# The expert's second matrix as one sum of 512 columns, and a second layer that starts with the high parts

## The reference

```python
def expert_block(args):
    xblk, e = args
    return (jax.nn.silu(xblk @ w1[e]) * (xblk @ w3[e])) @ w2[e]
```

## Time and profile before

| what | value |
|---|---|
| median of 3 runs | 950.17 us (949.08 to 951.76) |
| span of the profiled execution | 950.5 us |
| PE busy | 890.4 us, 94% |
| DVE busy | 633.5 us, 67% |
| ACT busy | 404.7 us, 43% |
| POOL busy | 196.5 us, 21% |
| PE on the chain that ended last | 43% of the span |
| passes of 256 columns for the second matrix | 1104, about 0.28 us each as shown, overlapping |
| weight loads | 48 of 2 MB, 13.7 us from issue to landing (median) |

### The profile page before, as it was taken

One profiled execution on the slowest core, in us unless ns is written; L12 is line 12 of the kernel. 1 busy time (PEld: TensorE's weight loads), 2 busy tenths in 40 slices (PEclk: granted clock), 3 DMA queues, 4 the chain that ended last, 5 costly groups with the idle time before them and its releaser, 6 DMA issues.

```text
span 950.5 us, 15781 instructions
## 1 busy us (share of the span) xinstructions
PE 890.4 (94%) x5739; PEld 756.8 (80%) x5740; DVE 633.5 (67%) x876; ACT 404.7 (43%) x559; POOL 196.5 (21%) x216
## 2 busy tenths in 40 slices
PE   4989999999999999999999999999999999999880
PEld 1788877888897577887888988988898898888770
DVE  1567555689867547455875759499845746799934
ACT  3573375301224432221421556377543533677721
POOL 4231000000000010110001323233513313244233
PEclk9898999999999999999979999999999999999985
DMA  9845445502034033122947769889989669699765
GB/s 340 308 139 160 140 134 174 181 13 68 20 134 178 3 131 111 67 90 89 335 172 249 248 181 335 270 270 378 377 260 326 198 177 307 196 356 359 284 210 221
DMA packets 81254, 194.55 MB, mean 205 GB/s; under 512 B 4043, under 2 KB 12400, under 8 KB 81211
## 3 DMA queue, kind: packets, MB, share of 16 engines
q1 hardware_dynamic: 70624, 158.87, 47.6%
q0 software_dynamic: 7712, 25.10, 10.7%
q10 hardware_dynamic: 2874, 10.01, 2.7%
HBM read 168.53 MB, written 25.71 MB: 204 GB/s over the span
## 4 chain that ended last, share of the span: by engine, by line
PE 43%; DVE 4%; DMA 2%; issue 1%; ACT 1%; POOL 0%; DVEq 0%; ACTq 0%; POOLq 0%; SPq 0%
PE ps L2019 26%; PE ps L2030 9%; PE ps L2035 4%; PE ps L2013 2%; DMA raw<-in_w_dram 2%; DVE arena L1601 1%; PE ps L2002 1%; PE ps L2069 1%; PE ps L2048 0%; PE ps L1953 0%; DMA out_dram<-arena 0%; DVE onehot L1506 0%; DVE w1l L1542 0%; ACT arena L1062 0%; PE ps L1998 0%
## 5 line engine op out<-in xcount | busy, mean ns | idle before, releaser
L2019 PE MATMUL ps<-w3h,xTh 128*128 128x256 f32 x368 | 105.9, 288 | 0.0
L2019 PE MATMUL ps<-w3h,xTl 128*128 128x256 f32 x368 | 104.1, 283 | 0.0
L2019 PE MATMUL ps<-w3l,xTh 128*128 128x256 f32 x368 | 104.1, 283 | 0.0
L1542 DVE TENSOR_TENSOR w1l<-raw,w1h 128x2048 fp32r<-128x2048 f32 x30 | 68.6, 2287 | 28.4 <-ACT w1h L988 28.4
L988 ACT ACTIVATE w1h<-raw 128x2048 fp32r (+1 forms) x32 | 61.1, 1912 | 57.9 <-PE ps L2035 39.4
L2019 PE MATMUL ps<-w2h,hTh 128*128 128x512 f32 x184 | 76.9, 418 | 1.0 <-DVE hTl L1555 0.5
L2030 PE MATMUL ps<-w1h,xTh 128*128 128x512 f32 x184 | 73.0, 397 | 3.7 <-issue 3.4
L988 ACT ACTIVATE w2h<-raw 128x2048 fp32r (+1 forms) x32 | 61.1, 1918 | 31.5 <-PE ps L2019 22.7
L2030 PE MATMUL ps<-w1l,xTh 128*128 128x512 f32 x184 | 72.8, 395 | 0.0
L2019 PE MATMUL ps<-w2l,hTh 128*128 128x512 f32 x184 | 72.2, 393 | 0.0
L2019 PE MATMUL ps<-w2h,hTl 128*128 128x512 f32 x184 | 72.1, 392 | 0.0
(11 more groups left out here) (349 smaller groups left out, 2215.6 us busy)
## 6 DMA issues: line engine op xcount, KB each, us to landing
raw<-in_w_dram SPq DMA_DIRECT2D x48, 2048.0 KB, 13.7
arena<-in_w_mod_dram SPq DMA_DIRECT2D x32, 512.0 KB, 3.8
arena<-in_x_dram SPq DMA_DIRECT2D x16, 512.0 KB, 9.5
arena<-in_w_in_dram SPq DMA_DIRECT2D x8, 1024.0 KB, 6.3
arena<-in_w_mod_dram SPq DMA_DIRECT2D x3, 2048.0 KB, 13.5
x_rows<-arena ACTq DMA_DIRECT2D x9, 512.0 KB, 3.2
hx_rows<-arena ACTq DMA_DIRECT2D x9, 512.0 KB, 4.2
wo_f<-in_w_out_dram SPq DMA_DIRECT2D x2, 2048.0 KB, 8.6
```

The costliest lines, as they stand in the source:

```text
L1542: dve.tensor_tensor(half_of(j, w_lo[j][:, :], k), half_of(j, raw[:, bass.ds(base, UNIT)], k), half_of(j, w_hi[j][:, :], k).bitcast(F32), A ...
L2019: ins = pe.matmul(out_ap, parts[l][:, lhs], w_parts[w][:, cols], start=start and n == 0, stop=stop and n == 2)
```

## The change

- The second matrix becomes one sum of 512 columns into bank 3: 24 passes instead of 48. `l1b` is now given when half of the depth is through, `l1c` when all is. w3 is split by halves of the depth, as w1 and w2 are.
- Both halves of the product of gate and up wait for `l1c`. Both now read bank 3.
- PE turns six tiles of the next rows, waits for the first half of `hid`, turns it (bank 5), turns the last two tiles, and waits for `hTh_a` (the high part) instead of `hT_a`.
- The second layer goes by halves of its depth: eight passes on the high part of `hid`, then (in the first half) the turns of the second half of `hid` into bank 4, then four passes on its low part.
- DVE makes in a splitting block low(0) for both halves, then both products, then both low parts of the turned half, and only then low(1, first half). ACT copies the two turned halves around `turn_out` and the second half of w3 behind both.

```diff
         def half_of(j, unit, k):
-            if j == 1:
-                return unit.rearrange("p (k n) -> p k n", k=KC)[:, :, k * 256:(k + 1) * 256]
             return unit[:, k * (UNIT // 2):(k + 1) * (UNIT // 2)]
...
                             high(1, place[1] * UNIT, 0)
-                            hidden_high(b, 0)
                             act.wait_ge(S["l1c"], b + 1)
                             act.sem_inc(S["load_seen"], 1)
-                            high(1, place[1] * UNIT, 1)
+                            hidden_high(b, 0)
                             turn_out(b + 1)
                             hidden_high(b, 1)
+                            high(1, place[1] * UNIT, 1)
...
             def hidden(b, k):
                 if k == 0:
                     dve.wait_ge(S["silu_done"], b + 1)
-                dve.wait_ge(S["l1c" if k else "l1b"], b + 1)
-                dve.tensor_tensor(hid[:, k * 256:(k + 1) * 256], hsil[:, k * 256:(k + 1) * 256], ps[:, 3 + k, 0:256], ALU.mult)\
+                    dve.wait_ge(S["l1c"], b + 1)
+                dve.tensor_tensor(hid[:, k * 256:(k + 1) * 256], hsil[:, k * 256:(k + 1) * 256], ps[:, 3, k * 256:(k + 1) * 256], ALU.mult)\
                     .then_inc(S["hid_b" if k else "hid_a"], 1)
...
                             low(0, place[0] * UNIT, e + 1, 0)
+                            low(0, place[0] * UNIT, e + 1, 1)
                             hidden(b, 0)
-                            low(0, place[0] * UNIT, e + 1, 1)
+                            hidden(b, 1)
                             hidden_low(b, 0)
-                            hidden(b, 1)
+                            hidden_low(b, 1)
                             low(1, place[1] * UNIT, e + 1, 0)
-                            hidden_low(b, 1)
                             turn_out(b + 1)
                             low(1, place[1] * UNIT, e + 1, 1)
                             weigh(b, s, pair)
...
             for k in range(2):
                 hidden(last, k)
+            for k in range(2):
                 hidden_low(last, k)
...
                 for q, done in enumerate(("l1b", "l1c")):
-                    for k in range(KC):
-                        if k == 0:
-                            pe.wait_ge(w_split[1], 2 * e + (q + 1))
-                        col = k * HALF + q * 256
-                        ins = product(ps[:, 3 + q, 0:256], x_parts, slice(k * P, (k + 1) * P), (w3h, w3l),
-                                      slice(col, col + 256), k == 0, k == KC - 1)
-                        if q == 1 and k == 3:
-                            pe.wait_ge(S["hid_a"], b + 1)
-                            for m in range(2):
-                                h_ins = pe.transpose(ps[:, 5, m * P:(m + 1) * P], hid[:, m * P:(m + 1) * P], ident[:, :])
-                            h_ins.then_inc(S["hta"], 1)
+                    pe.wait_ge(w_split[1], 2 * e + (q + 1))
+                    for k in range(4 * q, 4 * q + 4):
+                        ins = product(ps[:, 3, :], x_parts, slice(k * P, (k + 1) * P), (w3h, w3l),
+                                      slice(k * HALF, (k + 1) * HALF), k == 0, k == KC - 1)
                     ins.then_inc(S[done], 1)
                 if more:
-                    turn_block(b + 1)
-                pe.wait_ge(S["hT_a"], b + 1)
+                    turn_block(b + 1, 0, 6)
+                pe.wait_ge(S["hid_a"], b + 1)
+                for m in range(2):
+                    h_ins = pe.transpose(ps[:, 5, m * P:(m + 1) * P], hid[:, m * P:(m + 1) * P], ident[:, :])
+                h_ins.then_inc(S["hta"], 1)
+                if more:
+                    turn_block(b + 1, 6, KC)
+                pe.wait_ge(S["hTh_a"], b + 1)
                 pe.wait_ge(S["y_ready"], y_count)
-                for k in range(4):
-                    if k % 2 == 0:
-                        pe.wait_ge(w_split[2], 2 * e + (k // 2 + 1))
-                    if k == 2:
-                        pe.wait_ge(S["hT_b"], b + 1)
-                    for h in range(2):
-                        col = k * D + h * HALF
-                        ins = product(ps[:, 6 + h, :], h_parts, slice(k * P, (k + 1) * P), (w2h, w2l),
-                                      slice(col, col + HALF), k == 0, k == 3)
-                    if k == 1:
-                        ins.then_inc(S["l2_half"], 1)
-                    if k == 0:
+                for k0 in (0, 2):
+                    pe.wait_ge(w_split[2], 2 * e + (k0 // 2 + 1))
+                    if k0 == 2:
+                        pe.wait_ge(S["hTh_b"], b + 1)
+                    for k in range(k0, k0 + 2):
+                        for h in range(2):
+                            for w in (w2h, w2l):
+                                pe.matmul(ps[:, 6 + h, :], hTh[:, k * P:(k + 1) * P], w[:, k * D + h * HALF:k * D + (h + 1) * HALF],
+                                          start=(k == 0 and w is w2h), stop=False)
+                    if k0 == 0:
                         pe.wait_ge(S["hid_b"], b + 1)
                         for m in range(2):
-                            h_ins = pe.transpose(ps[:, 5, (2 + m) * P:(3 + m) * P], hid[:, (2 + m) * P:(3 + m) * P], ident[:, :])
+                            h_ins = pe.transpose(ps[:, 4, m * P:(m + 1) * P], hid[:, (2 + m) * P:(3 + m) * P], ident[:, :])
                         h_ins.then_inc(S["htb"], 1)
+                    pe.wait_ge(S["hT_b" if k0 else "hT_a"], b + 1)
+                    for k in range(k0, k0 + 2):
+                        for h in range(2):
+                            ins = pe.matmul(ps[:, 6 + h, :], hTl[:, k * P:(k + 1) * P], w2h[:, k * D + h * HALF:k * D + (h + 1) * HALF],
+                                            start=False, stop=(k == 3))
+                    if k0 == 0:
+                        ins.then_inc(S["l2_half"], 1)
                 ins.then_inc(S["l2_done"], 1)
```

More of the change, by code:

```diff
@@ L1007, in hidden_high @@
                 act.wait_ge(S["htb" if k else "hta"], b + 1)
-                act.activation(hTh[:, k * 256:(k + 1) * 256], ps[:, 5, k * 256:(k + 1) * 256], ACT.Copy)\
+                act.activation(hTh[:, k * 256:(k + 1) * 256], ps[:, 5 - k, 0:256], ACT.Copy)\
                     .then_inc(S["hTh_b" if k else "hTh_a"], 1)
@@ L1554, in hidden_low @@
                 dve.wait_ge(S["hTh_b" if k else "hTh_a"], b + 1)
-                dve.tensor_tensor(hTl[:, cols], ps[:, 5, cols], hTh[:, cols].bitcast(F32), ALU.subtract)\
+                dve.tensor_tensor(hTl[:, cols], ps[:, 5 - k, 0:256], hTh[:, cols].bitcast(F32), ALU.subtract)\
                     .then_inc(S["hT_b" if k else "hT_a"], 1)
@@ L2008, in _, with turn_block @@
             pe.sem_inc(S["y_ready"], 2)
-            def turn_block(b):
-                pe.wait_ge(S["gathered"], 16 * b + 16)
-                for k in range(KC):
+            def turn_block(b, first=0, end=KC):
+                if first == 0:
+                    pe.wait_ge(S["gathered"], 16 * b + 16)
+                for k in range(first, end):
                     ins = pe.transpose(ps[:, k // 4, (k % 4) * P:(k % 4 + 1) * P], xg[:, k * P:(k + 1) * P], ident[:, :])
-                ins.then_inc(S["x_turned"], 1)
+                if end == KC:
+                    ins.then_inc(S["x_turned"], 1)
             def product(out_ap, parts, lhs, w_parts, cols, start, stop):
```

## The result

The changed kernel takes 977.55 us (median of 4 runs, 975.86 to 980.5) against 950.23 us (949.08 to 951.76): ratio 1.028, 95% interval 1.026 to 1.031, so 27 us slower. The forecast was 972.5, 958 to 985. The profiled execution has a span of 974.0 us, and its own device time was 975.86, the lowest of the four. In every run that lists both, of either kernel, the device time is 1.7 to 1.9 us above the span. So the profiled execution before, span 950.5, took some 952.3 us by an estimate from these runs, 2 us over its median, and the spans differ by 23.5 us where the medians differ by 27.3.

What follows compares the result with a forecast made beforehand. PE, DVE and weight loads were nearly level in the runs; DVE would then pace eight rounds. Span 950.5 +14.7 +2.1 -0.5 +1.8 +4.4 = 973.0, so 972.5 us of device time, range 958 to 985.

Steps and rivals of the forecast that it cites:

- DVE's serial round: Between two splitting blocks DVE's in-order work takes 4.13 + 16.02 = 20.15 us against 18.31 now; eight times, +14.7 us.
- PE's own rounds: Where nothing else binds, a round is 18.30 us; seven rounds that split nothing grow 0.3 each, +2.1 us.
- The tail: Last block: the second copy comes 9.42 us after the second sum's start, was 7.61; final norm's squares follow it, +1.8 us.
- block 21's wait: Block 21's extra PE wait of 0.50 us, going back to a late w3, goes away: -0.5 us.
- The clock: PE's waits in the eight rounds drop the granted clock in every second one, at 1.1 us each: +4.4 us.
- Span and device time: From a span of 973.0 us, 0.3 off and the last halves rounded down gave 972.5 us of device time.
- (a): Rival: PE goes on setting the pace and DVE keeps up, all rounds 18.3, 953.6 us; chance 0.10.
- (c): Rival: the half clock becomes the rule, drops hit all high passes, 981 and up to 988 us; chance 0.12.
- The pass price: Second matrix: a 512-column pass costs 0.227 us by the rows, so 24 take 5.44, a gain of 0.31 per block.
- (b): Rival: PE's waits close as well, a round is PE's bare 17.63, 939 to 942 us; chance 0.07 together with (d).
- (d): Rival: the reordering does nothing, only 0.31 us a block is gained, 943 us; chance 0.07 together with (b).
- What I made of the formula: Second matrix: by the skill's formula the gain would be 0.06 us, and the sum 22 x 0.25 = 5 us higher.

Runs made afterwards that it cites:

- experiment 1: The changed kernel with the first w3 split on DVE moved between the two low parts of the turned half: 957.81 us, ratio 1.008 to the kernel before.
- experiment 5: The kernel before with two lines of DVE's order exchanged, the first w3 split behind the second low part: 962.06 us, ratio 1.012.
- experiment 6: The changed kernel once more, unaltered, for a second profile: 978.32 us, span 974.7.
- experiment 3: The kernel before with only the second layer's passes on the high parts first, two sums and DVE's and ScalarE's orders kept: 947.92 us, ratio 0.9964.
- experiment 2: The changed kernel with the second layer's passes in the old order, waiting for the low part first: 980.94 us, ratio 1.031 to the kernel before.
- experiments 4: The changed kernel with the second half's split of w1 moved behind the two products of gate and up: 963.05 us, ratio 1.012 to the kernel before.

## Why the prediction was right, step by step

**DVE's serial round.** Confirmed, by taking it away (experiment 1) and by making it alone (experiment 5). It was worked out as 4.13 + 16.02 = 20.15 us and is 4.32 + 16.13 = 20.45 in the round shown, 20.34 to 20.48 in all eight. The term was 8 x 1.84 = 14.7, each round going from 18.31 to 20.15. The rounds show +15.8, and it would be +16.8 if one of them (19.22) hadn't held 0.9 us of late weights before, which the term left out. I was 0.19 short on the way to the second low part: the eight high passes take 1.93 us from the first's start to the turns behind them (664.21 to 666.14) where I had 8 x 0.227 = 1.81, and ScalarE's copy starts 0.48 behind turns that followed a wait, not 0.41.

**PE's own rounds.** The mechanism is right, the size was too small: 18.53 us, not 18.30. By the starts of its instructions in the round of block 10, the way from the product to the first high pass takes 1.58 us where I had 1.49, and from there to the end of the second layer's first half it is 3.05 (703.10 to 706.15) where I had 1.81 + 0.22 + 0.91 = 2.94: the passes start again behind a wait, and I priced them as in a full stream. Over thirteen rounds that is +5.1 instead of the 2.1 of the sum. This is the term that was most off in share.

**The tail.** Expected +1.8 for the last block, and -0.5 for block 21's wait, together +1.3; measured from block 21's product on +1.8. It hangs on another thing than I said, though. ScalarE's timeline in the changed kernel, answering to the earlier trace rows:

```profile
941.78 0.38 ACT L1006 ACTIVATE hTh<-ps 128x256 fp32r<-128x256 f32 x1 [2.59 <-PE ps L2067]
942.41 1.06 ACT L1060 ACTIVATE arena<-arena 128x1024 f32<-128x1024 f32 x1 [0.24 <-DMA arena<-x_rows]
...
947.40 1.06 ACT L1060 ACTIVATE arena<-arena 128x1024 f32<-128x1024 f32 x1 [1.08 <-DMA arena<-x_rows]
```

The squares wait for the rows' landing, not for the copy. By the chain of waits, that landing goes back over the adding of block 21's rows (10.74 us of transfer) to its weighing on DVE, which stands ten microseconds behind the block's product, behind two splits of w3. That the sizes are near each other is chance. In experiment 6, the same kernel, this stretch is only 0.6 us longer than before, with 9.81 us for that transfer; in experiment 1, with the same last block, it is 1.1 us shorter (58.2), and there the squares start behind the copy without a wait.

**The clock.** Four falls at 1.1 us were taken; the two profiles show one each behind the eight waits, at 1.6 and 1.5. The price of a fall that meets the high passes was right at its upper end, the number too high: 2 of 16 waits of some 1.8 us were followed by one, and 2 of 8 of some 1.35 with one of 0.9 behind them. The Trainium skill (TensorE: Matmul & The Clock Gate, HAM oscillation) tells of a kernel whose clock fell in every tile, but behind waits of 3 to 5 us. The trace agrees with it where PE stands idle that long, between blocks 21 and 22:

```profile
923.72 0.77 PE L2031 MATMUL ps<-w1h,xTh 128*128 128x512 f32 x1 [3.29 <-issue]
```

There the granted clock is 0.50, the 1.2 GHz level, from 923.0 to 929.8, and all eight profiles have such a fall at this place. The timed runs of the changed kernel lie 1 to 4.6 us above its profiled one, with mean granted clocks of 0.964 to 0.969 against 0.976. That mean takes in the other stages and doesn't tell of falls in the rounds: the profile of experiment 6 has 0.968 with one fall there, that of the kernel before 0.964 with none. Whether the slower runs hold more falls stays open.

**Span and device time.** I put the device time 0.3 us under the span, because I held the span of one execution against the median of others. It stands 1.7 to 1.9 above the span in every run, 1.86 in the profiled one. That alone is 2.2 of the 5.0 us between forecast and median; 1.7 more is that the profiled execution was the fastest of its four. The span itself was forecast at 973.0 and is 974.0. Its errors mostly cancel: -0.8 on where the stage begins, +1.1 on the eight rounds, +3.0 on the others, -2.8 on the clock, +0.5 behind block 21's product. So that the span came within 1 us is luck; that DVE paces the eight rounds isn't.

**The rivals.** PE keeping the pace (a) holds in the thirteen other rounds and fails in the eight. The half clock as the rule (c) fails: seven of eight waits in each profile pass without a fall. (b) and (d) fail: the wait for the copy shows as 10.5 us idle on PE ahead of the first high passes, x184, in the page's group of L2062. The pass price taken from the rows holds, 5.44 for 24. The formula of the Trainium skill (TensorE: Matmul & The Clock Gate, Back-to-back issue gap) gives 215.8 ns for 512 columns, and the chain shows 227. The same section has about 131 ns for 512 columns in a stream with its weight loads; no pass here comes near that. What I made of the formula was also counted wrong: 22 x 0.25 is 5.5, and only the fourteen rounds that DVE doesn't pace could carry it, 3.5 us.

**What the change is made of.** The single sum gains 0.31 us of passes per block and loses the cover of the product, copy and turn. Even with DVE's order mended, the kernel with the single sum is 957.8 against 951.7 (experiment 1), and 9.9 us above experiment 3, which has the high parts first but two sums and the old orders: 18.53 us a round against 18.00. No run has the single sum alone. The high parts first gain 3.8 us on the kernel before (experiment 3) and 2.6 or 3.4 on the changed one (experiment 2). DVE's order loses some 20 us (experiment 1), falls of the clock among it. The part worth keeping is the second one, at 947.9 us.

## What to carry to other kernels

An engine that works 17.4 us of an 18.3 us round has under 1 us to spare, even when it is not on the chain. Add up its in-order work from the last wait that hangs on the leading engine to the next thing that engine needs. If a reordering removes work from ahead of such a wait, that sum grows by the removed piece, although no busy time changes. Joining the two sums into one saved 0.31 of 5.75 us of passes here, and took away the work that hid the way from the first sum's result back to the matrix engine.

## What the runs showed of the hardware

Whether the granted clock falls behind a wait of PE goes with the wait's length, and isn't sure for the middle ones. Where PE stood idle for 3.0 to 3.35 us, between blocks 21 and 22, it fell in all eight profiles. Of 16 waits of 1.7 to 1.9 us with four turns and a second wait of 0.5 behind them, two were followed by 3.4 us at the 1.2 GHz level; of 8 of 1.3 to 1.4 us with a second wait of 0.9, two as well. Of the 13 of 0.97 to 1.58 us in experiments 4 and 5, none was.

Eight passes behind a wait take 1.90 to 1.94 us from the first one's start to the next group's, where they take 1.81 in a full stream (experiments 1, 4 and 6 and the changed kernel, falls of the clock left out). So a wait of PE costs 0.1 us more than its own length here.
